# Row swaps of the differential queries and keys on GpSimd's queue, and the S5 input matrices made in two blocks with the first unit one block later

## What is computed

```python
qkv = u @ w_qkv
q, k, v = jnp.split(qkv, 3, axis=-1)
q = apply_rope_2(rms_norm_2(q, q_gain), cos, sin) * (HEAD_DIM ** -0.5)
k = apply_rope_2(rms_norm_2(k, k_gain), cos, sin)
...
def apply_rope_2(t, cos, sin):
    t1, t2 = jnp.split(tf, 2, axis=-1)
    out = jnp.concatenate([t1 * c - t2 * s, t2 * c + t1 * s], axis=-1)
```

```python
a_bar = jnp.exp(lam * dt)
b_bar = ((a_bar - 1.0) / lam)[..., None] * b_mat
...
bu = jnp.einsum('sgh,gph->sgp', u_row.astype(jnp.complex64), b_bar[r])
```

## Time and profile before

| | us |
|---|---|
| median of three runs | 3257.51 |
| lowest, highest | 3255.71, 3260.61 |
| profiled execution, its time | 3260.06 |
| profiled execution, span from first to last instruction | 3258.2 |
| TensorE products (PE) busy | 2914.1 (89%) |
| DVE busy | 1692.5 (52%) |
| ACT busy | 1090.2 (33%) |
| GpSimd (POOL) busy | 57.2 (2%) |
| the queue of SP's DMAs, share of 16 engines | 25.1% |

### The profile page before, as it was taken

How to read it: one execution, slowest core, us unless ns; L and a number is a source line. 1 busy time by engine, 2 the same in 40 slices (tenths; PEclk the granted TensorE clock), 3 DMA queues, 4 the chain that set the end, 5 groups by cost and what they waited for, 6 DMA issues and landing times.

```text
span 3258.2 us, 38782 instructions
## 1 busy us (share of the span) xinstructions
PE 2914.1 (89%) x14906; PEld 2351.5 (72%) x14906; DVE 1692.5 (52%) x2444; ACT 1090.2 (33%) x1540; POOL 57.2 (2%) x42
## 2 busy tenths in 40 slices
PE   3999989999886789899999998798999875989998
PEld 2798768887674467778787776577887655778787
DVE  5566565655542556543333446748677373443342
ACT  2312333222322434433222444633232333343231
POOL 1003000000000000000000000000000000000000
PEclk7999999999896789799999999999999987999999
DMA  5550344555433000013332332024434544123232
GB/s 184 166 157 1 106 136 131 163 142 142 151 117 119 1 1 1 1 53 99 100 91 84 100 101 68 1 68 103 147 136 155 209 115 91 52 85 96 90 103 65
DMA packets 448551, 320.11 MB, mean 98 GB/s; under 512 B 14002, under 2 KB 435996, under 8 KB 448412
## 3 DMA queue, kind: packets, MB, share of 16 engines
q1 hardware_dynamic: 328592, 237.00, 25.1%
q10 hardware_dynamic: 119820, 81.18, 8.5%
HBM read 292.00 MB, written 19.86 MB: 96 GB/s over the span
## 4 chain that ended last, share of the span: by engine, by line
PE 73%; DVE 12%; ACT 4%; DMA 4%; issue 4%; ACTq 1%; POOL 1%; SPq 0%; DVEq 0%; POOLq 0%
PE ps L435 49%; PE ps L417 6%; PE ps L429 3%; PE ps L843 2%; DMA ada_ring<-in_ada_w 2%; DVE ada_ring L493 1%; DMA nsa_area<-nsa_area 1%; DVE ada_ring L1682 1%; PE ps L2533 1%; PE ps L829 1%; PE ps L816 1%; PE ps L1591 1%; PE ps L1556 1%; DVE ada_first L507 1%; DVE h_area L1686 1%
## 5 line engine op out<-in xcount | busy, mean ns | idle before, releaser
L435 PE MATMUL ps<-hh,whi 128*128 128x512 f32 x1744 | 690.6, 396 | 9.1 <-DVE wlo L389 4.8
L435 PE MATMUL ps<-hh,wlo 128*128 128x512 f32 x1744 | 681.4, 391 | 0.0
L435 PE MATMUL ps<-hl,whi 128*128 128x512 f32 x1744 | 680.9, 390 | 0.0
L389 DVE TENSOR_TENSOR wlo<-raw,whi 128x2048 fp32r<-128x2048 f32 x198 | 453.7, 2292 | 309.6 <-ACT whi L385 309.6
L385 ACT ACTIVATE whi<-raw 128x2048 fp32r<-128x2048 f32 x198 | 377.3, 1905 | 423.3 <-PE ps L435 255.9
L435 PEld LDWEIGHTS ps<-hh,whi 128*128 128x128 f32 x1744 | 329.0, 189 | 85.5 <-issue 11.1
L435 PEld LDWEIGHTS ps<-hl,whi 128*128 128x128 f32 x1744 | 329.0, 189 | 70.3 <-issue 3.1
L435 PEld LDWEIGHTS ps<-hh,wlo 128*128 128x128 f32 x1744 | 328.5, 188 | 68.8
L435 PE MATMUL ps<-hid_h,whi 128*128 128x512 f32 x756 | 306.2, 405 | 7.6 <-DVE wlo L389 7.6
L435 PE MATMUL ps<-hid_h,wlo 128*128 128x512 f32 x756 | 299.7, 396 | 0.0
L435 PE MATMUL ps<-hid_l,whi 128*128 128x512 f32 x756 | 299.5, 396 | 0.0
(11 more groups left out here) (397 smaller groups left out, 4311.5 us busy)
## 6 DMA issues: line engine op xcount, KB each, us to landing
raw<-in_ffn_w_in SPq DMA_DIRECT2D x44, 1024.0 KB, 6.0
ada_ring<-in_ada_w ACTq DMA_DIRECT2D x80, 512.0 KB, 4.0
raw<-in_ffn_w_up SPq DMA_DIRECT2D x32, 1024.0 KB, 5.3
raw<-in_ffn_w_down SPq DMA_DIRECT2D x32, 1024.0 KB, 5.8
raw<-in_ffn_w_out SPq DMA_DIRECT2D x32, 704.0 KB, 4.6
raw<-in_hgrn_w_in SPq DMA_DIRECT2D x16, 1024.0 KB, 6.0
raw<-in_attn_w_qkv SPq DMA_DIRECT2D x12, 1024.0 KB, 6.5
s_area<-cp_dram SPq DMA_DIRECT2D x6, 2048.0 KB, 10.4
```

What stands on the lines that cost most here:

```text
L389: nc.vector.tensor_tensor(wlo[:, par, :], raw[:, par, :], whi[:, par, :].bitcast(F32), ALU.subtract).then_inc(w_lo, 1)
L435: m = nc.tensor.matmul(ps[:, bank, :], tile(w, kt, j), x[:, kt, :], start=(kt == 0 and n == 0), stop=(kt == k - 1 and n == 2))
```

## The change

The swaps go from SP's queue to GpSimd's and are issued there back to back for the eight pairs, ahead of `diff_pool`. Two semaphores of their own, one for even and one for odd pairs, take the place of two that were reused. A swap now waits for its block's evacuation and, from the third on, for the rotation of the pair two before it (before: from the fifth on, of the pair four before it, whose slots it takes). The S5 step of block 5 is split: two of its six operations stay and four go to block 6. The first unit moves from block 6 to block 7, and block 28 carries two units instead of one, so that each unit before it comes one later in the order. The two semaphores of the output are now those of the parameter columns, with their counts moved on.

```diff
-        out_rdy, stored, out_ps = sem("out_rdy"), sem("stored"), sem("out_ps")
+        out_rdy, stored, out_ps = cols_rdy, sem("stored"), cols_ps
...
-        turned_in = ((g_in, CMP_LOADS), (nsa_in, 80))
+        turned_in = ((sem("turned_even"), 0), (sem("turned_odd"), 0))
...
-        def d_turn(sp, db):
-
-            sp.wait_ge(ev_a, seg["d_q"].ea0 + 2 * db + 2)
-            if db >= 4:
-                sp.wait_ge(dn_rot, RP0 + 2 * db - 6)
+        def d_turn(pool, db):
+
+            pool.wait_ge(ev_a, seg["d_q"].ea0 + 2 * db + 2)
+            if db >= 2:
+                pool.wait_ge(dn_rot, RP0 + 2 * db - 2)
             slots = slice(2 * db % 8, 2 * db % 8 + 2)
             for row in range(0, P, 32):
-                sp.dma_start(d_rot[row:row + 32, slots, :], d_pair(db)[row ^ 32:(row ^ 32) + 32, :, :]
+                pool.dma_start(d_rot[row:row + 32, slots, :], d_pair(db)[row ^ 32:(row ^ 32) + 32, :, :]
                              ).then_inc(turned_in[db % 2][0], 16)
...
-        PER_BLOCK = [0] * 6 + [1, 1] + [1, 2, 1, 2, 1, 2, 1, 2] + [1] * 8 + [2, 1, 2, 1, 1, 1, 1, 1]
+        PER_BLOCK = [0] * 7 + [1] + [1, 2, 1, 2, 1, 2, 1, 2] + [1] * 8 + [2, 1, 2, 1, 2, 1, 1, 1]
...
             elif gb == 5:
-                tmp = tmp5.rearrange("p (h g) -> p h g", h=GH)
                 dve.wait_ge(s5_pp, 4)
                 tt(by_g(b_bar[:, 0, :, :]), taken(4), wide(wr), ALU.mult)
                 link(tt(by_g(b_bar[:, 1, :, :]), taken(4), wide(wi), ALU.mult))
+            elif gb == 6:
+                tmp = tmp5.rearrange("p (h g) -> p h g", h=GH)
                 dve.wait_ge(s5_pp, 5)
                 link(tt(tmp, taken(6), wide(wi), ALU.mult))
...
-                elif s.name in D0:
-                    for b in range(s.n):
-                        load(b, (s.g0 + b) % 2, True)
-                        if D0[s.name] + b >= 4:
-                            d_turn(sp, D0[s.name] + b - 4)
...
-            sp.wait_ge(out_rdy, 2 * TT)
+            sp.wait_ge(out_rdy, 2 * TT + 1)
...
             if upto >= 9:
+                for db in range(8):
+                    d_turn(pool, db)
                 diff_pool(pool)
...
-                dve.wait_ge(out_ps, n + 1)
+                dve.wait_ge(out_ps, n + 3)
...
-                    pe.wait_ge(out_rdy, n - 3)
+                    pe.wait_ge(out_rdy, n - 2)
```

## The result

In the first comparison the changed kernel took 3241.18 us (median of six runs, 3233.95 to 3242.05) against 3256.61 us for the kernel before (3253.11 to 3260.61): ratio 0.9948, 95% interval 0.9935 to 0.9961. Two more comparisons of the same pair gave 0.9924 (0.9912 to 0.9936) and 0.9935 (0.9917 to 0.9953). So the change makes the kernel faster by 17 to 25 us. The forecast of 25.3 us stands just above the upper end of that. The profiled execution took 3241.54 us with a span of 3239.7, against 3260.06 and 3258.2 before. In all comparisons one execution stood far off, 4240.51 us at a mean granted clock of 0.641, in the variant with swaps early on SP's queue; medians and ratios leave it out.

A forecast was written before the change was run, and what follows sets the result against it. TensorE's weight products were taken to bound the kernel, stalled by late row swaps and by a wait for the first S5 unit; 19.5 + 5.8 = 25.3 us off the median 3257.51 gave 3232.2 us, range 3227 to 3243.

The forecast's parts named there:

- The closed loop: Differential projections: swaps issued behind the load waiting for `wlo` of block b+2; one turn 15.8 us against TensorE's 12.62.
- 19.5 us forecast for this part: Differential projections: with swaps on GpSimd's queue the last product starts near 1973.8, not at 1993.27.
- landing time L: Differential blocks: time until a group of four swaps issued from GpSimd has landed, taken as 8.6 us, low end 4.1.
- 18.2 us were allowed: Differential blocks: a swap issued 1.4 us after a block's products end may take 18.2 us before TensorE's products are late.
- first rival (A): Differential blocks: GpSimd's issue slow or starved, swap over 18.2 us, some 10 us given back, 3242; chance 0.12.
- the one on the other side (C): Differential blocks: swaps from GpSimd worse than from SP, landing above about 28 us, total about 3272; chance 0.04.
- Part 2: First MLP of the second part: S5 matrices in two blocks, units one block later, 5.8 us less.
- slow products: Start of `mlp0_out0`: products slower after TensorE's wait of 3 us, by 1.2 to 2.6 us, taken as 1.9.
- turning that the prediction called owed: MLP: one S5 unit's turning on TensorE, 0.9 us, still to be paid, bringing 6.7 us down to 5.8.
- row tile with 1.7 us to spare: First block of `mlp0_out0`: 15th of 16 row tiles, from block 7's squares, ready by 2275.0, asked for at 2276.7.
- rival B: MLP: stall moves to block 7's squares or block 28, nothing of 5.8 us is left, 3238; chance 0.08.
- Rival D: Differential blocks: nothing moves, L near 26 or blocks held by ACT's high half or the weight load, 3256; chance 0.05.

The follow-up runs named there:

- swaps-only run: Changed kernel with the S5 part taken back, swaps still on GpSimd's queue: 3237.98 us, ratio 0.9936 against the kernel before.
- delay run: Changed kernel, each swap group also waiting until TensorE has finished the next block's products, GpSimd's queue otherwise empty: 3237.38 us.
- S5 run: Kernel before with the S5 part alone, swaps still on SP's queue: 3254.06 us, ratio 0.998.

## Why the prediction was right, and where it was off

Forecast: 3232.2 us, range 3227 to 3243. The three medians are 3241.18, 3234.74 and 3236.03; all lie in the range and all above the forecast, the first near its upper end. All three are faster by more than 0.2%. The mechanism was right in both parts; that the first median lies in the range is in part luck (see below).

**The closed loop** was the cause of the first stall. L1088's idle time fell from 69.6 to 4.8 us, TensorE's five waits for `wlo` are gone, and steps are 12.62 us. The swaps-only run wins the 19.5 us forecast for this part as 19.3 in its stage and 20.9 by its ratio (0.0064 x 3261).

**The landing time L** was put at 8.6 us. In the changed kernel L1088 starts 4.3 to 4.7 us after the first issue in six of the seven groups that it waits for and 5.4 in the other, and the issue comes 0.3 after evacuation: 4.6 to 5.7. The price came from a row in which the swaps stood right behind a 1 MB load. In the changed kernel the next load is issued at 1897.55, at the end of the `wlo` that starts at 1895.07 and 4.0 us after the swap. The term was mis-sized by a third to a half and changed nothing, because 18.2 us were allowed. It did mislead the other way round in the delay run: there I carried the fast landing over to a place beside a load, where 8.6 was the right number.

**GpSimd's queue** was the first rival (A) and the one on the other side (C). The Trainium skill, "SBUF — State Buffer", section "Who interferes with whom", gave the caution that DVE could hold up GpSimd's descriptors. The changed kernel hardly puts that to the test, since DVE is idle during the first three of four issues in most groups. The run late by one block does: a `wlo` subtraction starts at 1884.65 and lasts 2.28 us, four issues start at 1885.04 under it, take 1.93 us as they do beside an idle DVE, and land in 4.8. So this operation doesn't hold GpSimd's issues up; for others of DVE no run here shows it. The Trainium skill's "DMA: Bandwidth & Descriptors", section "Anatomy of one DMA — SWDGE (gpsimd) path", gave an estimate of 2.3 us for one; the median here is 2.7.

**Part 2** was forecast as 5.8 us and measures 6.2 to 6.5 in its stage, 6.5 by the ratio of the S5 run (0.002 x 3259), though with an interval of 2.9 to 10.1 us. Its terms: the wait 3.0 forecast, 2.90 measured. The slow products 1.9 forecast, about 1.6 measured: the turning and what else lies before the next product took 1.62 us (2268.81 to 2270.43) where 0.87 was full speed, and the block 12.91 (2270.43 to 2283.34) where 12.08 was. The granted clock shows why, here first of the changed kernel and then of the kernel before. The first row of each holds the wait and the turning, the second the block behind them:

```profile
2265.80:2270.40 4.60, 1.70 (x9) 1.59 (x9) 4.57 (x7) 1.91 (x1) 0.00 (x0) 0.83 0.79 228
2270.40:2282.60 12.20, 12.20 (x51) 9.73 (x50) 4.86 (x7) 1.09 (x2) 0.00 (x0) 0.92 0.41 130
```

```profile
2266.90:2276.70 9.80, 1.75 (x10) 1.65 (x9) 8.56 (x12) 4.08 (x6) 0.00 (x0) 0.68 0.38 108
2276.70:2289.80 13.10, 13.10 (x51) 10.42 (x50) 6.89 (x9) 2.94 (x4) 0.00 (x0) 0.85 0.39 120
```

The one unit's turning that the prediction called owed came due at 2405.80 us of the changed kernel, where the first kind's last unit is turned a block later: 0.9 us, as forecast. The row tile with 1.7 us to spare was in time (TensorE has no wait in the first block of `mlp0_out0`), and rival B, which rested on it and on block 28, is out: the S5 run alone keeps its 6.3 us. Rival D is out with the swaps-only run. Two slips of the prediction change nothing: it speaks once of four waits of TensorE where the rows have five, and D's 3256 leaves out part 2, with which it would be 3252.

**What the sum left out** is the scatter between executions. By stages the change wins 19.3 + 6.4 = 25.7 us against one run of the kernel before, or some 24 against the mean of those that share the stage (-2.2 and -0.2, -1.7 and -0.3 in the table). The three comparisons say 17, 25 and 21 us. The range held because its upper end was drawn for rivals A and B, and the spread of "some 3" us put into it was too small: six or more runs of one kernel spread over 8 to 16 us here. That is the luck in it.

Two of the three places where the scatter arises show the same thing, TensorE's granted clock behind a wait. On entering attention TensorE waits 2.0 us for DVE in every run. Here is the changed kernel behind that wait, and then the swaps-only run:

```profile
1982.20:1995.70 13.50, 11.14 (x32) 5.17 (x30) 9.59 (x15) 6.97 (x19) 0.00 (x0) 0.50 0.23 78
```

```profile
1979.00:1982.20 3.20, 2.71 (x8) 0.69 (x4) 3.17 (x4) 0.14 (x1) 0.00 (x0) 0.50 0.04 12
1982.30:1995.70 13.40, 9.84 (x58) 5.93 (x60) 10.97 (x20) 10.07 (x28) 0.00 (x0) 1.00 0.22 75
```

One stays at 0.50, the level of 1.2 GHz, for over 13 us, the other is back at 1.00, that of 2.4 GHz, after little more than 3. The five runs with +2.0 to +2.2 in the attention column are all of the first kind; those from -1.2 to 0.0 have only a short stretch at 0.50, like the second. The kernel before shows both, one in each of its two runs, so the edit doesn't decide it. In the S5 layer the two runs with +4.2 and +4.3 have a stretch of some 10 us at 0.50 that the others lack (in the second run of the kernel before, 2590.3 to 2600.3). And the 1.7 us of that run in the MLP go with a clock that was at 0.50 for some 7 us behind the wait, where the first run's was for some 10. What decides how long the clock stays low after the same wait isn't settled. Nor are the shifts before the differential blocks, nor why one comparison's ratio comes out 8 us from another's.

## What to carry to other kernels

An issue that has its data, but stands in a queue behind one that waits for something later, can close a loop through three engines; it is the place in the queue that matters, not whose queue it is, and moving it ahead of the waiting one on the same queue brings as much. Work out how late a transfer may be before deciding how fast it must be, and ask separately for latency (which overlaps over as many blocks as lie between issue and use) and for occupancy of the in-order queue (which doesn't overlap, and has to stay under one block). And when a change of 0.7% is judged, compare the touched stage between two traces: here it repeated within 0.3 us in three runs while the gain by the totals moved by 8.

## What the runs showed of the hardware beyond that

- A swap group's landing depends on what is in flight: from the first of GpSimd's issues to the rotation, mostly 4.3 us and up to 5.6 with no 1 MB load issued in the 4 us before it or the 2 after it; 5.9 to 6.3 behind a load by 1.6 to 1.9 us, 7.0 by 0.9, 8.3 to 8.6 by 0.3 to 0.5; 7.7 and 9.3 with a load 1.5 and 0.9 us after the first issue. SP's took 8.4 us in the earlier trace rows. Which queue issues it matters less: 0.48 us per issue and a median of 2.7 us to landing from GpSimd, 0.6 us and 2.3 from SP.
- TensorE products after a wait: behind 3.66 us idle the granted clock of the next 7.9 us was 0.78 (a mix of the levels 1.2 and 2.4 GHz), then 1.00; behind 2.90 us it was 0.92 over the next block. That wait cost some 1.6 us on top of itself. On entering attention, with a wait of 2.0 us in both, the kernel before took 2.0 us longer in one execution than in the other, with 0.50 granted for a longer stretch.
